# Buffers placed by address modulo 256 bytes, shift columns split inside a down projection, and attention scores from rounded pairs

## The reference, cut to what matters

```python
def reference(x, ..., ctx_2, ...):
    x = first_block(x, ...)          # 2 layers: attention + SSD mixer, then a gated FFN
    return second_block(x, ...)      # layer 0: hyena + mLSTM, layer 1: latent attention (MLA); conv FFNs

def second_block(x, c, ctx, ...):
    for layer in range(2):
        h_lat = rmsnorm(x_lat, norm_mix[layer]) * (1 + sc1) + sh1      # sh1: the shift columns
        h_ctx = rmsnorm(x_ctx, norm_mix[layer]) * (1 + csc1) + csh1
        ...
def mla_mixer(h_ctx, h_lat, ...):
    qa, kva, kr = mla_down(h, w_down)                  # latents: 384 + 256 + 64 channels
    q_n, q_r = split(rmsnorm(qa, q_norm) @ w_uq)       # per head: 128 plain channels + 64 turned by rope
    k_n, v   = split(rmsnorm(kva, kv_norm) @ w_ukv)    # per head: 128 + 128
    k_r      = rope(kr)                                # one set of 64 channels for all 8 heads
    s = (q_n . k_n + rope(q_r) . k_r) * 192 ** -0.5    # 512 queries (4 blocks of 128) x 768 keys
    y = (softmax(s) @ v) @ w_o
```

## Time and profile before

| | us |
|---|---|
| median of 3 runs | 3497.31 |
| lowest and highest | 3497.17, 3501.21 |
| profiled execution, its own time | 3496.98 |
| its span, first to last instruction | 3494.9 |
| mean granted TensorE clock, share of full speed | 0.949 |
| PE busy | 3213.5 (92% of the span) |
| DVE busy | 1856.3 (53%) |
| ACT busy | 1105.9 (32%) |

### The profile page before, as it was taken

One profiled execution on the slowest core, in us unless ns is written; L12 is line 12 of the kernel. 1 busy time (PEld: TensorE's weight loads), 2 busy tenths in 40 slices (PEclk: granted clock), 3 DMA queues, 4 the chain that ended last, 5 costly groups with the idle time before them and its releaser, 6 DMA issues. The chain is left out here.

```text
span 3494.9 us, 40088 instructions
## 1 busy us (share of the span) xinstructions
PE 3213.5 (92%) x16222; PEld 2681.5 (77%) x16222; DVE 1856.3 (53%) x2810; ACT 1105.9 (32%) x1634; POOL 101.0 (3%) x78
## 2 busy tenths in 40 slices
PE   8989999999889999999685869999999779999998
PEld 5667888876678888899562359999999754489897
DVE  5745766757457777565364335543553224356464
ACT  4433322234433223333350013221222233333232
POOL 0030000000210000000000010000000000000000
PEclk9988999999989999999896889999999889999999
DMA  3100544421005555121000021121122010032232
GB/s 120 49 25 31 189 149 165 158 69 49 30 19 178 189 173 173 59 97 67 19 1 23 37 84 62 66 68 58 62 72 86 24 52 1 0 115 97 92 99 82
DMA packets 74226, 278.42 MB, mean 80 GB/s; under 512 B 7899, under 2 KB 12507, under 8 KB 72636
## 3 DMA queue, kind: packets, MB, share of 16 engines
q1 hardware_dynamic: 74044, 275.87, 23.7%
HBM read 267.45 MB, written 8.39 MB: 79 GB/s over the span
## 5 line engine op out<-in xcount | busy, mean ns | idle before, releaser
L122 PE MATMUL banks<-normed_hi,weights_hi 128*128 128x384 f32 (+2 forms) x2672 | 891.4, 340 | 14.5 <-DVE normed_lo L1019 14.5
L123 PE MATMUL banks<-normed_lo,weights_hi 128*128 128x384 f32 (+2 forms) x2672 | 888.9, 339 | 0.0
L104 ACT ACTIVATE weights_hi<-weights_raw 128x1024 fp32r<-128x1024 f32 (+3 forms) x365 | 395.8, 1084 | 1279.0 <-PE banks L125 1229.7
L125 PE MATMUL banks<-normed_hi,weights_lo 128*128 128x384 f32 (+2 forms) x2672 | 747.0, 339 | 0.0
L110 DVE TENSOR_TENSOR weights_lo<-weights_raw,weights_hi 128x1024 fp32r<-128x1024 f32 (+3 forms) x365 | 460.4, 1261 | 171.1 <-ACT weights_hi L104 167.4
L122 PEld LDWEIGHTS banks<-normed_hi,weights_hi 128*128 128x128 f32 x2672 | 503.5, 188 | 47.3 <-DVE normed_lo L1019 15.2
L123 PEld LDWEIGHTS banks<-normed_lo,weights_hi 128*128 128x128 f32 x2672 | 505.7, 189 | 32.3
L125 PEld LDWEIGHTS banks<-normed_hi,weights_lo 128*128 128x128 f32 x2672 | 473.2, 190 | 32.2
L123 PE MATMUL banks<-hidden_lo,weights_hi 128*128 128x512 f32 (+1 forms) x880 | 323.0, 367 | 0.0
L122 PE MATMUL banks<-hidden_hi,weights_hi 128*128 128x512 f32 (+1 forms) x880 | 323.0, 367 | 0.0
L125 PE MATMUL banks<-hidden_hi,weights_lo 128*128 128x512 f32 (+1 forms) x880 | 294.8, 367 | 0.0
(11 more groups left out here) (375 smaller groups left out, 4233.9 us busy)
## 6 DMA issues: line engine op xcount, KB each, us to landing
weights_raw<-in_w_up SPq DMA_DIRECT2D x176, 512.0 KB, 3.5
ada_tiles<-in_ada SPq DMA_DIRECT2D x96, 512.0 KB, 3.5
weights_raw<-in_w_down SPq DMA_DIRECT2D x64, 704.0 KB, 4.0
weights_raw<-in_w_in SPq DMA_DIRECT2D x67, 512.0 KB, 3.5
weights_raw<-in_w_out SPq DMA_DIRECT2D x32, 512.0 KB, 3.5
x_kept<-x SPq DMA_DIRECT2D x2, 3072.0 KB, 11.2
x<-x_kept SPq DMA_DIRECT2D x1, 3072.0 KB, 9.8
weights_raw<-in_mla_down SPq DMA_DIRECT2D x6, 512.0 KB, 3.5
```

The source lines that it names most:

```text
L104: act.activation(self.hi[:, n % 2, 0:w], self.raw[:, n % 2, 0:w], ACT.Copy).then_inc(self.high_ready, 1)
L122: pe.matmul(out, self.hi[:, s, m], xh, start=k == 0, stop=False)
L123: pe.matmul(out, self.hi[:, s, m], xl, start=False, stop=False)
L125: mm = pe.matmul(out, self.lo[:, s, m], xh, start=False, stop=k == kt - 1)
```

## The change

**1. Places.** The buffers of `Ring`, `split_pair`, `x`, the movable buffers (`Places`) and those of `mla` start at multiples of 256 bytes (PHASE), where they started at multiples of 32 or 64. On the addresses this has these effects. The pair `normed` moves from 192 modulo 256 to 0 (196544 to 196352 for the 512-column form, 179136 to 178944 for the 784-column form). `x`, `consts`, `rope` and `vectors` move from 128 to 0. Of the plain float32 operands, gates, decay rows and scaled C tiles move from 192 to 0. The weights and the pairs `hidden`, `mixed`, `attention`, `ssd` and `latents` lie at 0 before and after.

**2. Shift columns.** The `Shifts` of the second block's first layer is given to the last down projection of the first block. ACT and DVE do their parts at tile 4 of its 8 tiles, and only PE's wait (`ShiftsThere`) stays in its old place. The other three `Shifts` stay as they are.

**3. The last attention.** The query stage evacuates its 8 head tiles as pairs into `mixed` (ACT high, DVE low), and DVE copies the 4 rope tiles. The key stage evacuates as pairs too, high over `x`, low into `keys_lo`. `turn_rope` takes the place of `head_norm_rope`: it turns the keys first, then splits the turned keys, and stacks for each head the high part of its 64 query channels and the low part into one tile of 128 rows. The V projection comes ahead of the key projection. Each piece of scores is now five fp32r matmuls: keys_hi x q_hi, keys_lo x q_hi, keys_hi x q_lo, rope_keys_hi x stacked (128 rows; both halves of rope_keys hold the same channels), and rope_keys_lo x q_hi (64 rows).

```diff
-        self.hi = ctx.enter_context(nc.sbuf_tensor("weights_hi", [P, 2, UNIT], F32R))
+        self.hi = ctx.enter_context(nc.sbuf_tensor("weights_hi", [P, 2, UNIT], F32R, align_bytes=PHASE))
...
-    with nc.sbuf_tensor(unique(name + "_hi"), [P, tiles, tokens], F32R, align_bytes=LINE) as hi, \
+    with nc.sbuf_tensor(unique(name + "_hi"), [P, tiles, tokens], F32R, align_bytes=PHASE) as hi, \
...
@@ Residual.scalar, Residual.vector
             if H or self.squares:
                 self.done(act, j)
+            if self.shifts and j == 4:
+                self.shifts.scalar(act)
...
             if j:
                 follow(j - 1)
+            if self.shifts and j == 4:
+                self.shifts.vector(dve)
...
@@ Plain
     def scalar(self, act):
         for j in range(self.n):
-            act.wait_ge(Z.R.product, self.first + j + 1)
-            act.activation(self.home[:, j], Z.slot(...), ACT.Copy).then_inc(Z.evacuated, 1)
+            if j < self.paired:
+                act.wait_ge(Z.R.product, self.first + j + 1)
+                act.activation(self.pair[0](j), self.product(j), ACT.Copy).then_inc(Z.hi_made, 1)
             Z.R.high(act, self.first + j + 2)
     def vector(self, dve):
         for j in range(self.n):
-            self.Z.R.rest(dve, self.first + j + 2)
+            if j < self.paired:
+                dve.wait_ge(Z.hi_made, self.hi0 + j + 1)
+                dve.tensor_tensor(self.pair[1](j), self.product(j), self.pair[0](j).bitcast(F32),
+                                  ALU.subtract).then_inc(Z.evacuated, 1)
+            else:
+                dve.wait_ge(Z.R.product, self.first + j + 1)
+                dve.tensor_copy(self.rest[:, j - self.paired], self.product(j)).then_inc(Z.evacuated, 1)
+            Z.R.rest(dve, self.first + j + 2)
...
@@ turn_rope, new
+                act.wait_ge(turned, 1)
+                act.activation(keys_hi, keys, ACT.Copy).then_inc(rope_hi, 1)
+                for n in range(4):
+                    act.wait_ge(turned, n + 2)
+                    for m, r in enumerate(rows):
+                        last = act.activation(stacked[r, 2 * n + m], queries[r, n], ACT.Copy)
+                    last.then_inc(rope_hi, 1)
...
+                def low(n):
+                    dve.wait_ge(rope_hi, n + 1)
+                    if n == 0:
+                        dve.tensor_tensor(keys_lo, keys, keys_hi.bitcast(F32), ALU.subtract).then_inc(rope_lo, 1)
+                        return
+                    for m, r in enumerate(rows):
+                        last = dve.tensor_tensor(stacked[rows[1 - m], 2 * n - 2 + m], queries[r, n - 1],
+                                                 stacked[r, 2 * n - 2 + m].bitcast(F32), ALU.subtract)
+                    last.then_inc(rope_lo, 1)
+                for n, x in enumerate(tiles):
...
+                    if n:
+                        low(n - 1)
+                low(4)
...
@@ mla
-        Z.run(Plain(Z, 12, own.operand(H, first=CTX), own, q))
-        head_norm_rope(nc, K, [(q[:, 8 + n], None) for n in range(4)] + [(kr[:, LAT], None)])
-        Z = Line(nc, K, R, 0)
-        both = form_of(SEGS)
-        Z.run(Plain(Z, 8, both.operand(H, 3), both, kn))
+        Z.run(Plain(Z, 12, own.operand(H, first=CTX), own, lambda j: Hm[0][:, j], lambda j: Hm[1][:, j], qr, 8))
+        turn_rope(nc, K, qr, kr[:], qs, krh[:], krl[:], free)
...
+        Z = Line(nc, K, R, 0)
+        both = form_of(SEGS)
+        Z.run(Plain(Z, 8, both.operand(H, 3), both, kh, lambda j: kl[:, j]))
...
         def parts(h, q0):
-            r = 64 * (h % 2)
-            return [(q[:, h, q0:q0 + P], lambda a, w: kn[:, h, a:a + w]),
-                    (q[r:r + 64, 8 + h // 2, q0:q0 + P], lambda a, w: kr[r:r + 64, a:a + w])]
+            r = slice(64 * (h % 2), 64 * (h % 2) + 64)
+            qh, ql = (x[:, h, q0:q0 + P] for x in Hm)
+            return [(qh, kh(h)), (qh, kl[:, h]), (ql, kh(h)), (qs[:, h, q0:q0 + P], krh),
+                    (qs[r, h, q0:q0 + P], krl[r])]
...
@@ Places, and the first down projection's caller
-        self.base = (nc.sbuf_base + LINE - 1) // LINE * LINE
+        self.base = (nc.sbuf_base + PHASE - 1) // PHASE * PHASE
...
-                more = dict(last=[Finish(Z, c, mod, gains, fine_gain[:])], twice=norm2)
+                shifts = Shifts(Z, H2, shift(0, 0))
+                more = dict(last=[Finish(Z, c, mod, gains, fine_gain[:])], twice=norm2, shifts=shifts)
...
-        Z.run(*stages, Shifts(Z, H2, shift(0, 0)),
+        Z.run(*stages, ShiftsThere(shifts),
```

More of the change, by code:

```diff
@@ L238, in at, with norm_split @@
         return self.spread[:, n, 0:self.segs[n][1]]
-def norm_split(nc, K, src, pair, k0, segs, tiles, size, gain, shift=None, keep=None, sums=None):
+def norm_split(nc, K, src, pair, k0, segs, tiles, size, gain, h, shift=None, keep=None, sums=None):
     hi, lo = pair
@@ L1176, with __init__ @@
 class Plain(Stage):
-    def __init__(self, Z, tiles, rhs, form, home):
-        self.Z, self.n, self.rhs, self.form, self.home = Z, tiles, rhs, form, home
+    def __init__(self, Z, tiles, rhs, form, high, low, rest=None, paired=None):
+        self.Z, self.n, self.rhs, self.form = Z, tiles, rhs, form
+        self.pair, self.rest, self.paired = (high, low), rest, tiles if paired is None else paired
         self.first, self.t0 = Z.take_tiles(tiles)
+        self.hi0 = Z.take("hi_made", self.paired)
     def sync(self, sp):
@@ L1185, in sync, with product @@
             self.Z.R.load(sp, self.first + j + 2)
+    def product(self, j):
+        return self.Z.slot(self.t0 + j, self.form.base, self.form.total)
     def tensor(self, pe):
@@ L1217, in head_norm_rope, with _ @@
         pr = ctx.enter_context(nc.psum_tensor(unique("rope_ps"), [P, 2, 512], F32))
-        if with_norm:
-            sq = ctx.enter_context(nc.sbuf_tensor(unique("squares"), [P, 2, SEQ], F32))
-            rc = ctx.enter_context(nc.sbuf_tensor(unique("rstd_cols"), [P, N * LT, 2], F32))
-            pn = ctx.enter_context(nc.psum_tensor(unique("norm_ps"), [P, 256, 2], F32))
-            pb = ctx.enter_context(nc.psum_tensor(unique("rstd_ps"), [P, 2, 512], F32))
-        with stage(nc, "squares_ready", "sums_ready", "root_ready", "inverted", "spread", "normed", "swapped", "dve_step",
-                   "done") as (
-                block, squares_ready, sums_ready, root_ready, inverted, spread, normed, swapped, dve_step, done):
+        with stage(nc, "swapped", "rope_step", "turned", "rope_hi", "rope_lo") as (
+                block, swapped, rope_step, turned, rope_hi, rope_lo):
+            tiles = [keys[:, LAT]] + [queries[:, n] for n in range(4)]
+            @block.tensor
+            def _(pe):
+                for n, x in enumerate(tiles):
+                    if n >= 2:
+                        pe.wait_ge(turned, n - 1)
+                    pe.matmul(pr[:, n % 2], K["swap"], x, start=True, stop=True).then_inc(swapped, 1)
@@ L1326, in scores @@
                         for m, (q, k) in enumerate(parts):
-                            mm = pe.matmul(ps[:, n % 2, b, 0:w], q, k(a, w), start=m == 0,
+                            mm = pe.matmul(ps[:, n % 2, b, 0:w], q, k[:, a:a + w], start=m == 0,
                                            stop=m == len(parts) - 1)
@@ L2956, in feed_forward @@
         down = Residual(Z, KT, rhs, X, segs, gate, scaled=conv is None, H=H2 if half else None, squares=bool(half),
-                        after=hidden, ada=down_ada and not half, twice=twice if half else None)
+                        after=hidden, ada=down_ada and not half, twice=twice if half else None,
+                        shifts=shifts if half else None)
         out += [up, *(last if half else ()), down]
```

118 lines of the change are left out of this document (38 added, 80 removed).

## The result

The changed kernel took 3454.77 us (median of 4 runs, 3451.08 to 3455.92) against 3497.24 us before (4 runs): a ratio of 0.9877, with a 95% interval of 0.986 to 0.9894. The profiled execution has a span of 3454.1 us, 40.8 less than before.

A forecast was written before the change was run, and what follows sets the result against it. PE, busy 92% of the span, was taken as the bound. Savings of 19 + 9.5 + 18 = 46.5 us from 3496.98 gave 3450.5, with 0.3 for the median 3451; range 3443 to 3459, or 3440 to 3472 with the 3470 rival.

The forecast's parts named there:

- FirstMix: 3 x 288 matmuls over `normed` gain 5.7 us if PE sets the pace; taken as 5.
- the saving on the scores: Last attention: scores per block from 3.26 to 2.43 us, 26.6 over 32 blocks, net 25.5 after 1 us of PE waiting.
- Part 1, 19: Moving `normed` from 192 to 0 modulo 256 quickens its 512-column matmuls: 19 us, bounds 0 and 19.6.
- The price of the Up stages: Up stages: 2112 matmuls of 512 columns over `normed` gain 6.6 ns each, 13.9 us.
- The deduction for PE's wait on the weights: In FirstMix PE waits for the weights' low part, 15.5 us idle, so 5.7 us was cut to 5.
- The rival that the place does nothing: `normed` is read at 233 ns for another reason; only 27.5 us go, time 3470; chance 0.26.
- The doubt from the earlier trace: 768-column stages use all four places, yet steps of k take 1.06 us each, with none standing out.
- Part 2, 9.5: Ahead of the second block's first projection, PE's 8.07 us of idle time go, plus 1.4 of clock: 9.5 us.
- the last k: Rival at the second block's first projection: the Shifts' wait returns there, PE stops within the first tile; 3459, chance 0.05.
- Part 3, 18: Last attention: 25.5 us saved on scores less 7.5 us paid in the stages before it, net 18 us.
- What is paid: Stages ahead of the attention: rope 7.5, query 0.6, key 1.8 less, barrier 1.2; sum 7.5 us, bounds 3 and 13.
- a rival for the whole attention: If PE waits in every block, the clock falls to the lower level; wholly there 3599 us; chance 0.02.

The follow-up runs named there:

- Part 1 alone: Only the buffer places of the change, applied to the kernel before: 3481.7 us against 3498.56, ratio 0.995.
- the first experiment: Each of the change's three parts put alone on the kernel before: 3481.7 us (places), 3487.26 us (shift columns), 3479.92 us (last attention).

## Why the prediction was right

The forecast was 3451 us, the result 3454.77, and all three parts gained by the mechanism that was worked out. Two terms were too large, FirstMix and the saving on the scores.

**Part 1, 19 against some 17.** The price of the Up stages was exact (13.9 us forecast and measured). FirstMix was to give 5: its second layer gave 3.1, and its first can't be told from its own spread of 4 us. The deduction for PE's wait on the weights had the wrong reason, as that wait is as long without the change; the matmuls there gained some 4 ns each where 6.6 was carried over from the Up stages. Part 1 alone gave 17 us between medians. The rival that the place does nothing is refuted by the first experiment. The doubt from the earlier trace rows is resolved as well: in the 768-column stages all distances occur, and their step of k stayed at 1.06 us. In single matmuls the distance does show there, in both directions (the low part's matmul of 386 columns takes 171 ns at distance 192 and 178 at 64, that of 384 takes 179 and 176), distance 0 is not the quickest of them, and the sum over the six of a step cancels most of it. The rule of the Trainium skill ("TensorE: Matmul & The Clock Gate", Part 2, "What happens when you issue a matmul"), that loading weights takes nothing from the moving operand's reads, would have given 3470. The runs don't agree that places cost nothing at 512 columns: 226.7 ns at distance 0, 233.3 at 192, by the addresses alone. Whether the two reads get in each other's way is not shown, since only the addresses were varied.

**Part 2, 9.5 against 9.7.** Between the last down projection and the second block's first tiles the changed kernel's lead grew from 15.5 to 25.2 us: 8.2 across the gap and 1.5 of clock. PE didn't stop at the last k either.

**Part 3, 18 against 14.2.** From the first query matmul to the end of the attention, 269.8 us became 255.6. What is paid was 6.2 us instead of 7.5 (rope stage 6.9 longer, key stage 1.7 shorter). The saving on the scores was 20.5 instead of 25.5, and this is the step that was mis-sized. The block as a whole came out as forecast, 3.15 to 3.19 us against 3.15, but with luck: its transposes took 0.63 and not 0.72, its scores 2.52 and not 2.43, and the two differences cancel. Over four blocks 21.03 us became 17.84, which times 8 is the 25.5 of the forecast. What I left out is the clock. I had put the evacuation of the last key tile and a barrier ahead of the attention and priced them as 1.2 us of time, but not asked what the 4.8 us of idle PE do: the granted clock was 0.50 for the first 11.27 us of the attention, where before it came up with the clock at 1.00 from the V projection, 1.80 us of idle PE ahead of it. The two groups of scores ahead of the first transposes took 8.74 us and the first block 4.31, about 5 us more than at the upper level. The prediction had named the clock as a rival for the whole attention, and not as a term at its start.

In the changed kernel's own trace the three are 15.5, 9.7 and 14.2 us, which is 39.4 of the 40.8 between the spans; the rest are small differences between and behind them. Part 1 has 15.5 there, since the first layer's FirstMix took 1.1 us longer than before.

## What to carry to other kernels

Put the stationary and the moving operands of a long stream of fp32r matmuls at the same address modulo 256: at 512 columns it was worth up to 3% of each matmul, at no cost; in the 768-column stages, whose rows run through all four places, it was worth nothing. A small operand of the next stage belongs into the stage ahead, in the middle of its tiles; behind the last tile it waits for everything queued there. Before PE's work on a stretch is cut, look at the next bound: here 2.93 us of DVE and ACT were 7% under 3.15, and only when other PE work was moved beside them did the cut pay in full.

## What the runs showed that was not expected

- The distance modulo 256 between a matmul's two operands in SBUF sets its spacing at 512 columns: 226.7 ns at 0, 229 on the mean of three at 64, 233 at 128 and at 192.
- A 64-row matmul among 128-row ones costs some 0.4 us beyond its own time (0.09 on the one ahead, 0.20 on itself, 0.11 on the one behind); the same product on 128 rows costs 0.174 in all.
- The same instructions behind a gap of 4.2 to 4.9 us got the upper clock back at very different times: 5.8, 8.0, 8.1, 11.1, 11.3, 11.9 and 12.3 us into the attention in seven traces, which alone is worth up to 3 us. Even behind a gap of 1.80 us, where it stayed up in three traces, it fell a microsecond into the attention in a fourth (the one with everything at 192) and cost 7 us.
- The first layer's FirstMix takes 339.6 to 343.7 us in kernels that differ in nothing there or in places only. A difference of 2 or 3 us between two traces is looked for there first.
